# Latent attention rounds: the order of the values' products, the projection piece and the reading of its bank

## The chip, the cores and the metric

The kernel runs on one core of one Trainium2 chip. The metric is the device time of one launch in microseconds (us); lower is better. The core has a matrix engine (TensorE, "PE" in the profile; its weight loads are "PEld"), VectorE (DVE), ScalarE (ACT), GpSimd (POOL) and SyncE (SP), which issues most of the DMAs. Each engine works through its own queue in order, and the engines wait for each other on semaphores. Matrix products land in PSUM, which has 8 banks of 512 fp32 columns.

## The reference

One launch computes two blocks on a sequence of 1024 tokens of 1024 features: a first block (a gated recurrence, a band attention, a feed-forward layer), and a second one (a recurrent layer, and then a latent attention). Only the latent attention matters here. Cut to what is needed:

```python
c_kv = rms_norm(ckr[..., :256], kv_norm)               # latent of keys and values
k_nope = einsum("bsc,chd->bshd", c_kv, w_uk)           # 8 heads of 128
v      = einsum("bsc,chd->bshd", c_kv, w_uv)           # 8 heads of 128
q = einsum("bsc,chd->bshd", c_q, w_uq)                 # 8 heads of 128 + 64; c_q has 384 features
q_rope = apply_rope(q[..., 128:], cos, sin)
s = (q_nope . k_nope + q_rope . k_rope) * ATTN_SCALE   # causal, in blocks of 128 queries
p = softmax(s)
y = (p @ v) * silu(gate)
out = x + y @ w_out
```

## The kernel before

The latent attention runs in 64 rounds, one for each head H = n // 8 and block of 128 queries. In a head the blocks go backwards: round r = n % 8 has 8 - r key blocks of 128 keys. The projections of keys, queries and values for two heads (a pair) are cut into 14 pieces, and the pieces of the next pair are spread over the rounds of the present one, as "fillers" between the products of the attention (`MLA_FILLERS`, line 70, `mla_fillers`, line 73). In an even head rounds 1 to 4 have one filler each: pieces 10 to 13. An odd head below 7 has one or two in every round: 14; 15 and 16; 17; 18; 19; 20; 21 and 22; 23. The last head has none. So four heads (0, 2, 4, 6) are of the even kind with fillers, and three (1, 3, 5) of the odd kind. Pieces 14 and 15 are the rotary part of the queries, 10, 11, 16 and 17 the other part of the queries, 12, 13, 18 and 19 keys, 20 to 23 values (counted from the pair's first piece; in the code m is that number plus 14 for each earlier pair).

Each engine has its order written out by hand (PE from line 1624, ACT from 2319, DVE from 3267). In round n:

- PE: `mla_transposed(n)` (line 1583, the weights of block n turned by nk transposes into banks 4 and 5); where there are two fillers, the first one; `mla_scores(n + 2)` (lines 1564 to 1573, into banks 0 and 1 or 2 and 3); the last filler, `mla_projection` (lines 1507 to 1509 and, for values, 1547 to 1549, into bank 7); `mla_values(n - 1)` (line 1593, into bank 6).
- DVE: `mla_probs_copied(n)` (line 3239, out of banks 4 and 5); the first of two fillers is read; `mla_max(n + 2)` (3228); `mla_read` of the last filler; `mla_inverse(n + 2)` (3233, a reciprocal of a sum that ACT forms in `mla_exp`); `mla_gated(n - 1)` (3250, out of bank 6). In rounds 2 and 3 of the odd heads `mla_rope_turned` follows (3214 to 3217), in round 4 of the odd and round 1 of the even heads `mla_rope_low` (2362, from the q_rope tile).
- ACT: in round 4 of the odd and round 1 of the even heads `mla_rope_high` (2281) goes first; the first of two fillers; `mla_exp(n + 2)` (2299); `mla_high` of the last filler (2274: it reads bank 7 and writes the rounded high part of a key or query piece; the pieces of values and of the rotary part have none); `mla_normed(n + 2)` (2305).

`mla_read` of a key or query piece (2362) waits for `mla_high` of that piece, since it forms the difference of bank and high part; of a value piece (3208) and a rotary piece (3199) it is a plain copy that waits for PE alone.

The waits that the change touches, all of PE:

```python
            def mla_projection(m):
                ...
                elif m >= 10:
                    pe.wait_ge(s_pread, m)
...
            def mla_transposed(n):
                pe.wait_ge(s_normed, n + 1)
                ...
                await_at_least(pe, mla.copied, n)
...
            def mla_values(n):
                pe.wait_ge(mla.copied, n + 1)
                await_at_least(pe, mla.outL, n)
```

`s_pread` counts the pieces that DVE has read: a piece from number 10 on goes into bank 7, and so waits until DVE has read the piece before it. `mla.copied` counts `mla_probs_copied`, and `mla.outL` counts `mla_gated`, so the values' product of block n waits until bank 6 has been read for block n - 1.

Of the kernel before, what the change touches and what calls it, by code (L numbers as in the profile page):

```python
# [72 lines left out]
def mla_fillers(n):  # L73

    H, r = n // 8, n % 8
    return [PIECES * (H // 2) + i for i in MLA_FILLERS[H % 2][r]] if H < 7 else []
# [129 lines left out]
def half_of(h):  # L206
    return slice(h * HALF, (h + 1) * HALF)
# [24 lines left out]
def await_at_least(eng, semaphore, count):  # L232

    if not isinstance(count, int) or count > 0:
        eng.wait_ge(semaphore, count)


def fused_kernel(nc, a):
    ctx = ExitStack()
    with ctx:  # L240
# [749 lines left out]
        def mla_key_columns(n):  # L990

            nk = mla.items[n][2]
            return 5 * P // 2 if nk == 5 else min(HALF, nk * P)
# [7 lines left out]
        def mla_bank(m):  # L1001
            return (4, 5, 6, 7, 0, 1, 4, 5, 6, 7)[m] if m < 10 else 7

        def mla_done(m):

            return MM_PER_UNIT * (K_UNIT + 3 * (m // PIECES)) + MLA_COUNT[m % PIECES]
# [12 lines left out]
        def _(pe):  # L1019
# [532 lines left out]
            def mla_scores(n):  # L1552
                H, j, nk = mla.items[n]
                e = H % 2
                if n % 8 < 2:
                    pe.wait_ge(s_pread, 6 if H == 0 else PIECES * (H // 2) + (PIECES if e else 6))
                await_at_least(pe, mla.probed, n - 1)
                queries = slice(j * P, (j + 1) * P)
                for b in range((nk + 3) // 4):
                    k0, k1 = b * mla_key_columns(n), min((b + 1) * mla_key_columns(n), nk * P)  # L1560
                    bank = 2 * (n % 2) + b
                    out = ps[:, bank, 0:k1 - k0]
                    diagonal = k1 == nk * P
                    nc.tensor.matmul(out, q_nopeH[:, e, queries], k_nopeH[:, e, k0:k1], start=True, stop=False)
                    nc.tensor.matmul(out, q_nopeL[:, e, queries], k_nopeH[:, e, k0:k1], start=False, stop=False)
                    nc.tensor.matmul(out, q_nopeH[:, e, queries], k_nopeL[:, e, k0:k1], start=False, stop=False)
                    if n % 8 < 2 and b == 0:
                        pe.wait_ge(s_qrL, H + 1)
                        pe.wait_ge(s_krL, 1)
                    nc.tensor.matmul(out, q_ropeS[:, e, queries], k_ropeH[:, 0, k0:k1], start=False, stop=False)  # L1570
                    last = nc.tensor.matmul(out, q_ropeS[:, e, queries], k_ropeL[:, 0, k0:k1], start=False, stop=not diagonal)
                    if diagonal:
                        last = nc.tensor.matmul(ps[:, bank, k1 - k0 - P:k1 - k0], ident_r[:], causal_r[:], start=False, stop=True)
                last.then_inc(mla.scored, 1)

            def mla_transposed(n):
                nk = mla.items[n][2]
                pe.wait_ge(s_normed, n + 1)
                if n == 0:
                    pe.wait_ge(s_pread, 8)  # L1580
                await_at_least(pe, mla.copied, n)
                for k in range(nk):
                    last = nc.tensor.transpose(transposed_flat[:, k * P:(k + 1) * P], mla.probs[:, n % 2, k * P:(k + 1) * P], ident[:])
                last.then_inc(mla.transposed, 1)

            def mla_values(n):
                H, _, nk = mla.items[n]
                if n % 16 == 0:
                    pe.wait_ge(s_pread, PIECES * (n // 16) + 10)
                pe.wait_ge(mla.copied, n + 1)  # L1590
                await_at_least(pe, mla.outL, n)
                for k in range(nk):
                    last = nc.tensor.matmul(ps[:, 6, 0:P], v_mla[H // 2 % 2][:, k, (H % 2) * P:(H % 2 + 1) * P],  # L1593
                                            mla.probsT[:, n % 2, k * P:(k + 1) * P], start=(k == 0), stop=(k == nk - 1))
                last.then_inc(mla.summed, 1)
# [10 lines left out]
            def output_chunks(r, first, last):  # L1606
                u, (_, tok) = STAGE["wob"][0] + r, output_half(r)
                if first == 0:
                    pe.wait_ge(s_split, u + 1)
                    if r > 4:  # L1610
                        pe.wait_ge(*output_read.at(r - 3))
                for k in range(first, last):
                    c = Y_ORDER[k]
                    if r % DC == 0:
                        pe.wait_ge(s_y7l, k + 1 + (r // DC) * 4 * (k >= 4))
                    wH, wL = w_high[:, u % 2, c * P:(c + 1) * P], w_low[:, u % 2, c * P:(c + 1) * P]
                    out = ps[:, output_bank(r)]
                    nc.tensor.matmul(out, wH, y7H[:, c, tok], start=(k == 0), stop=False)
                    nc.tensor.matmul(out, wH, y7L[:, c, tok], start=False, stop=False)
                    done = nc.tensor.matmul(out, wL, y7H[:, c, tok], start=False, stop=(k == DC - 1))  # L1620
                if last == DC:
                    done.then_inc(s_mm, MM_PER_UNIT)

            for n in range(64):
                fillers = mla_fillers(n)
                mla_transposed(n)
                if len(fillers) == 2:
                    mla_projection(fillers[0])
                if n + 2 < 64:
                    mla_scores(n + 2)  # L1630
                if fillers:
                    mla_projection(fillers[-1])
                if n:
                    mla_values(n - 1)
                if n >= 62:
                    output_chunks(0, 2 * n - 124, 2 * n - 122)
            mla_values(63)
# [722 lines left out]
        def _(dve):  # L2360
            def low_of(L, source, H):
                return nc.vector.tensor_tensor(L, source, f32(H), ALU.subtract)
# [830 lines left out]
            def mla_read(m):  # L3193

                p, i = m // PIECES, m % PIECES
                t, h, bank = i // 10, i % 2, ps[:, mla_bank(m)]
                if i in (0, 1):
                    dve.wait_ge(s_mm, mla_done(m))
                    nc.vector.tensor_copy(q_rope[:, half_of(i)], bank).then_inc(s_pread, 1)
                elif i in (2, 3, 10, 11, 4, 5, 12, 13):  # L3200
                    H, L = (q_nopeH, q_nopeL) if i in (2, 3, 10, 11) else (k_nopeH, k_nopeL)
                    dve.wait_ge(s_qnH, 8 * p + {2: 1, 3: 2, 4: 3, 5: 4, 10: 5, 11: 6, 12: 7, 13: 8}[i])
                    low_of(L[:, t, half_of(h)], bank, H[:, t, half_of(h)]).then_inc(s_pread, 1)
                else:
                    r = 2 * (i - 6)
                    dve.wait_ge(s_mm, mla_done(m))
                    await_at_least(dve, mla.summed, 16 * (p - 1))
                    nc.vector.tensor_copy(v_mla[p % 2][:, r:r + 2].rearrange("p r n -> p (r n)"), bank).then_inc(s_pread, 1)
# [37 lines left out]
            def mla_gated(m):  # L3246
                H, j, _ = mla.items[m]
                dve.wait_ge(mla.summed, m + 1)
                y = cgate[:, H, j * P:(j + 1) * P]
                nc.vector.tensor_tensor(y, ps[:, 6, 0:P], y, ALU.mult).then_inc(mla.outL, 1)  # L3250
# [16 lines left out]
            for n in range(64):  # L3267
                fillers = mla_fillers(n)
                H, r = n // 8, n % 8
                mla_probs_copied(n)  # L3270
                if len(fillers) == 2:
                    mla_read(fillers[0])
                if n + 2 < 64:
                    mla_max(n + 2)
                if fillers:
                    mla_read(fillers[-1])
                if n >= 62:
                    y_low_of(2 * n - 120)
                    y_low_of(2 * n - 119)
                if n + 2 < 64:  # L3280
                    mla_inverse(n + 2)
                if n:
                    mla_gated(n - 1)
                if H % 2 and H < 7 and r in (2, 3):
                    mla_rope_turned(H // 2 + 1, r - 2)
                if H % 2 == 0 and r == 1 or H % 2 and H < 7 and r == 4:
                    mla_rope_low(H + 1)
                if 57 <= n < 60 or n == 61:
                    y_low_of(min(n - 57, 3))
# [169 lines left out]
```

## Time and profile before

| | |
|---|---|
| median of 3 runs | 2532.97 us (2532.96 to 2535.27) |
| profiled execution, its own time | 2535.13 us |
| its span, first to last instruction | 2533.2 us |
| PE busy | 2484.3 us, 98% of the span |
| DVE busy | 1621.2 us, 64% |
| ACT busy | 946.6 us, 37% |
| chain that ended last | PE 82%, DVE 11%, ACT 3% |
| granted TensorE clock, mean | 0.996 of full speed |

Matmuls are pipelined: the record of one overlaps the start of the next, so the time from one start to the next is what counts on PE. The records of a 128-column fp32 product in line 1593 come in two passes (16 records for 8 key blocks).

### The profile page before, as it was taken

The numbers are of one execution on the slowest core, as the hardware profiler recorded it, in microseconds if no ns is written. First come the engines' busy times: TensorE is split into PE (matmuls) and PEld (weight loads), VectorE is DVE, ScalarE is ACT, GpSimd is POOL, SyncE is SP. The second block draws the span as 40 slices with busy tenths as digits, with TensorE's granted clock in tenths as the row PEclk, the third lists the DMA queues.
The fourth block names the chain that finished last, engine by engine and source line by source line (L and its number), as shares of the span: only waits on it lengthen the run. The fifth ranks groups of instructions, "written<-read, shape, count | busy, mean of one in ns | idle before, by whom it ended". The sixth has DMA issues, their size and how long they took to land.

```text
span 2533.2 us, 33765 instructions
## 1 busy us (share of the span) xinstructions
PE 2484.3 (98%) x13036; PEld 2071.5 (82%) x13036; DVE 1621.2 (64%) x1977; ACT 946.6 (37%) x1369; POOL 1055.7 (42%) x769
## 2 busy tenths in 40 slices
PE   8999999999999989999999999999999999999998
PEld 7878888887788878888878878888888888888887
DVE  6685723476655687667688796677784552556565
ACT  6252223222322343333345454346551331444432
POOL 3454523211243378888871113243345333111135
PEclk9999999999999999999999999999999999999999
DMA  3111121211341122222277521311132311110133
GB/s 143 45 35 34 47 72 42 71 39 47 130 165 62 55 75 75 84 92 75 84 210 195 152 68 67 112 42 41 49 116 75 133 67 49 29 29 10 34 117 125
DMA packets 65381, 201.96 MB, mean 80 GB/s; under 512 B 7136, under 2 KB 16480, under 8 KB 63840
## 3 DMA queue, kind: packets, MB, share of 16 engines
q1 hardware_dynamic: 52080, 152.85, 17.8%
q10 hardware_dynamic: 6256, 35.73, 3.7%
q0 software_dynamic: 6912, 11.54, 2.8%
q8 instruction: 91, 1.49, 0.2%
q14 instruction: 42, 0.34, 0.0%
HBM read 159.20 MB, written 32.51 MB: 76 GB/s over the span
## 4 chain that ended last, share of the span: by engine, by line
PE 82%; DVE 11%; ACT 3%; issue 2%; DMA 1%; POOL 1%; ACTq 0%; DVEq 0%; SPq 0%; POOLq 0%
PE ps L1034 8%; PE ps L1036 8%; PE ps L1035 8%; PE ps L1110 6%; PE ps L1112 5%; PE ps L1111 5%; PE ps L1373 5%; PE ps L1374 5%; PE ps L1375 5%; PE ps L1434 2%; PE ps L1436 2%; PE ps L1435 2%; PE ps L1593 2%; PE ps L1292 1%; PE ps L1309 1%
## 5 line engine op out<-in xcount | busy, mean ns | idle before, releaser
L767 POOL TENSOR_TENSOR derived_vectors<-w_staged 1x1 f32<-1x1 f32 x146 | 35.1, 240 | 1170.6 <-PE ps L1036 479.5
L772 POOL TENSOR_TENSOR w_low<-w_staged,w_high 128x1024 fp32r<-128x1024 f32 x146 | 390.3, 2673 | 11.4
L1110 PE MATMUL ps<-h_mix_high,w_high 128*128 128x512 f32 x688 | 278.5, 405 | 0.0
L1112 PE MATMUL ps<-h_mix_high,w_low 128*128 128x512 f32 x688 | 269.6, 392 | 0.0
L1111 PE MATMUL ps<-h_mix_low,w_high 128*128 128x512 f32 x688 | 269.3, 391 | 0.0
L1112 PEld LDWEIGHTS ps<-h_mix_high,w_low 128*128 128x128 f32 x688 | 129.7, 188 | 27.9
L1110 PEld LDWEIGHTS ps<-h_mix_high,w_high 128*128 128x128 f32 x688 | 130.0, 189 | 26.0 <-issue 0.2
L1111 PEld LDWEIGHTS ps<-h_mix_low,w_high 128*128 128x128 f32 x688 | 130.0, 189 | 25.2
L768 POOL CAST w_high<-w_staged 128x1024 fp32r<-128x1024 f32 x146 | 150.5, 1031 | 0.0
L1034 PE MATMUL ps<-h_rnn_high,w_high 128*128 128x512 f32 x320 | 124.6, 389 | 1.4 <-DVE h_rnn_low L2384 1.4
L2828 DVE TENSOR_TENSOR squares<-ps,squares 128x512 f32<-128x512 f32 x84 | 57.8, 689 | 106.3 <-PE ps L1375 105.6
L1035 PE MATMUL ps<-h_rnn_low,w_high 128*128 128x512 f32 x320 | 124.5, 389 | 0.0
L1036 PE MATMUL ps<-h_rnn_high,w_low 128*128 128x512 f32 x320 | 124.5, 389 | 0.0
L1434 PE MATMUL ps<-act_block_high,w_high 128*128 128x512 f32 x308 | 120.4, 391 | 2.0 <-DVE w_low L2759 1.4
L1436 PE MATMUL ps<-act_block_high,w_low 128*128 128x512 f32 x308 | 119.9, 389 | 0.0
L1435 PE MATMUL ps<-act_block_low,w_high 128*128 128x512 f32 x308 | 119.8, 389 | 0.0
L1881 ACT ACTIVATE probs_band<-ps,softmax_stats 128x640 f32<-128x640 f32 (+4 forms) x64 | 42.4, 663 | 142.1 <-DVE softmax_stats L2684 125.2
L2835 DVE TENSOR_TENSOR squares<-squares,rstd 128x512 f32<-128x512 f32 x66 | 90.8, 1378 | 3.9 <-ACT rstd L1692 1.8
L2299 ACT ACTIVATE probs_mla<-ps,softmax_stats 128x1024 f32<-128x1024 f32 (+3 forms) x64 | 47.5, 742 | 105.8 <-DVE softmax_stats L3228 97.9
L1593 PE MATMUL ps<-probs_mla_T,v_mla 128*128 128x128 f32 x576 | 76.0, 277 | 1.6 <-DVE mla_gate L3250 1.2
L1593 PEld LDWEIGHTS ps<-probs_mla_T,v_mla 128*128 128x128 f32 x576 | 71.8, 191 | 6.1 <-issue 3.1
L2690 DVE COPY probs_band_T<-ps 128x640 f32<-128x640 f32 (+4 forms) x64 | 42.1, 657 | 49.4 <-PE ps L1300 49.1
(632 smaller groups left out, 7084.2 us busy)
## 6 DMA issues: line engine op xcount, KB each, us to landing
w_staged<-weights_in SPq DMA_DIRECT2D x168, 512.0 KB, 3.5
w_staged_late<-weights_in SPq DMA_DIRECT2D x22, 512.0 KB, 4.3
gates_loaded<-gates ACTq DMA_DIRECT2D x8, 1024.0 KB, 7.2
gates<-tmp SPq DMA_DIRECT2D x16, 512.0 KB, 2.6
act_raw<-gates SPq DMA_DIRECT2D x16, 512.0 KB, 7.3
gates<-gates_staged_late SPq DMA_DIRECT2D x22, 256.0 KB, 2.0
x_in<-xT_in SPq DMA_DIRECT2D x8, 512.0 KB, 8.2
x_mid<-xT_in ACTq DMA_DIRECT2D x1, 4096.0 KB, 15.1
```

The lines of the kernel that those rows point to most:

```text
L768: nc.gpsimd.tensor_copy(w_high[:, j], w_staged[:, j]).then_inc(s_wh, 1)
L772: nc.gpsimd.tensor_tensor(w_low[:, j], w_staged[:, j], f32(w_high[:, j]), ALU.subtract).then_inc(s_split, 1)
L1034: nc.tensor.matmul(ps[:, bank], wH, rhs[0][:, r, tok], start=(n == 0), stop=False)
L1035: nc.tensor.matmul(ps[:, bank], wH, rhs[1][:, low_r, tok], start=False, stop=False)
L1036: last = nc.tensor.matmul(ps[:, bank], wL, rhs[0][:, r, tok], start=False, stop=last_chunk)
L1110: nc.tensor.matmul(ps[:, bank], wH, h1H[:, c, tok], start=(c == 0), stop=False)
L1111: nc.tensor.matmul(ps[:, bank], wH, h1L[:, c, tok], start=False, stop=False)
L1112: done = nc.tensor.matmul(ps[:, bank], wL, h1H[:, c, tok], start=False, stop=(c == DC - 1))
L1434: nc.tensor.matmul(ps[:, bank], wH[:, columns], H[:, c], start=not added and c == 0, stop=False, skip_group_check=added)
L1435: before_last = nc.tensor.matmul(ps[:, bank], wH[:, columns], L[:, c], start=False, stop=False, skip_group_check=added)
L1436: last = nc.tensor.matmul(ps[:, bank], wL[:, columns], H[:, c], start=False, stop=c == chunks - 1, skip_group_check=added)
L1593: last = nc.tensor.matmul(ps[:, 6, 0:P], v_mla[H // 2 % 2][:, k, (H % 2) * P:(H % 2 + 1) * P], mla.probsT[:, n % 2, k * P:(k + 1) * P], st ...
```

## The change

PE: the values' product of the block before follows the scores directly, and the last filler comes behind it, at the end of the round. DVE: the last filler is read behind the reciprocal and the gating, instead of ahead of them. ACT's order stays as it is: `mla_exp(n + 2)`, `mla_high` of the last filler, `mla_normed(n + 2)`. Where a round has two fillers, the first keeps its place on all three engines. `mla_rope_turned` and `mla_rope_low` follow the reading on DVE. No instruction is added or removed, and no wait is changed.

```diff
@@ PE @@
                 if n + 2 < 64:
                     mla_scores(n + 2)
+                if n:
+                    mla_values(n - 1)
                 if fillers:
                     mla_projection(fillers[-1])
-                if n:
-                    mla_values(n - 1)
                 if n >= 62:
                     output_chunks(0, 2 * n - 124, 2 * n - 122)
@@ DVE @@
                 if n + 2 < 64:
                     mla_max(n + 2)
-                if fillers:
-                    mla_read(fillers[-1])
                 if n >= 62:
                     y_low_of(2 * n - 120)
                     y_low_of(2 * n - 119)
                 if n + 2 < 64:
                     mla_inverse(n + 2)
                 if n:
                     mla_gated(n - 1)
+                if fillers:
+                    mla_read(fillers[-1])
                 if H % 2 and H < 7 and r in (2, 3):
                     mla_rope_turned(H // 2 + 1, r - 2)
```

## Rows read from the trace of the kernel before

**Rows 1.** Windows, heads 2 and 3: stretch, length, busy time by engine, PE clock.

```profile
2232.41:2263.66 31.25, 30.91 (x208) 28.14 (x206) 18.41 (x38) 15.63 (x29) 7.08 (x6) 1.00 0.08 24
2263.66:2306.28 42.62, 41.42 (x273) 37.56 (x273) 25.40 (x50) 16.63 (x30) 3.57 (x3) 1.00 0.10 26
```

**Rows 2.** Waits, all rounds: waiting, waited for, total us, times, longest.

```profile
PE ps L1547 <- DVE k_nope_low L2362: 2.8, 3, 0.9
```

**Rows 3.** Timeline, head 3, rounds 0 and 1: start, length, instruction.

```profile
2268.55 0.38 PE L1593 MATMUL ps<-probs_mla_T,v_mla 128*128 128x128 f32 x2
2268.75 0.69 DVE L3199 COPY q_rope<-ps 128x512 f32<-128x512 f32 x1 [1.19 <-PE ps L1509]
...
2269.50 0.50 PE L1507 MATMUL ps<-cq_high,w_high 128*128 128x512 f32 x1
```

**Rows 4.** Timeline, head 3, rounds 2 to 4: two turns, copies, ACT between them.

```profile
2282.68 0.71 PE L1583 MATMUL ps<-identity,probs_mla 128*128 128x128 f32 x5
...
2283.09 0.68 DVE L3214 TENSOR_TENSOR q_rope_rotated<-q_rope_rotated,cos_sin 128x512 f32<-128x512 f32 x1
...
2285.02 0.82 DVE L3239 COPY probs_mla_T<-ps 128x640 f32<-128x640 f32 x1
...
2286.91 0.59 ACT L2274 ACTIVATE k_nope_high<-ps 128x512 fp32r<-128x512 f32 x1
...
2287.53 0.69 DVE L2362 TENSOR_TENSOR k_nope_low<-ps,k_nope_high 128x512 fp32r<-128x512 f32 x1 [1.23 <-ACT k_nope_high L2274]
...
2290.32 0.68 DVE L3239 COPY probs_mla_T<-ps 128x512 f32<-128x512 f32 x1
2290.44 1.06 ACT L2281 ACTIVATE q_rope_split<-q_rope 64x1024 fp32r<-64x1024 f32 x1 [1.50 <-DVE q_rope L3217]
```

**Rows 5.** Timeline, head 3, rounds 4 to 6: up to piece 21.

```profile
2291.85 0.58 ACT L2274 ACTIVATE k_nope_high<-ps 128x512 fp32r<-128x512 f32 x1
...
2292.47 0.69 DVE L2362 TENSOR_TENSOR k_nope_low<-ps,k_nope_high 128x512 fp32r<-128x512 f32 x1 [1.13 <-ACT k_nope_high L2274]
2293.07 0.15 DVE L3233 RECIPROCAL softmax_stats<-softmax_stats 128x1 f32<-128x1 f32 x1
...
2293.45 1.22 DVE L2362 TENSOR_TENSOR q_rope_split<-q_rope,q_rope_split 64x1024 fp32r<-64x1024 f32 x1
...
2294.70 0.56 DVE L3239 COPY probs_mla_T<-ps 128x384 f32<-128x384 f32 x1
...
2295.98 0.17 DVE L3233 RECIPROCAL softmax_stats<-softmax_stats 128x1 f32<-128x1 f32 x1
...
2296.11 0.39 PE L1547 MATMUL ps<-w_high,ckv_high 128*128 128x256 f32 x1
...
2296.25 0.41 DVE L3239 COPY probs_mla_T<-ps 128x256 f32<-128x256 f32 x1
```

**Rows 6.** Timeline, head 2, round 1: the gating and the piece behind the scores.

```profile
2237.40 0.27 DVE L3250 TENSOR_TENSOR mla_gate<-ps,mla_gate 128x128 f32<-128x128 f32 x1
...
2237.66 0.45 PE L1507 MATMUL ps<-cq_high,w_high 128*128 128x512 f32 x1
```

**Rows 7.** Timeline, head 2: values behind a piece (round 2); rounds 5 and 6.

```profile
2245.59 1.72 PE L1593 MATMUL ps<-probs_mla_T,v_mla 128*128 128x128 f32 x14
...
2255.09 0.49 PE L1583 MATMUL ps<-identity,probs_mla 128*128 128x128 f32 x3
...
2256.98 0.38 PE L1583 MATMUL ps<-identity,probs_mla 128*128 128x128 f32 x2
```

**Rows 8.** Timeline, head 7: values behind scores, behind the gating, and line 1618 behind values.

```profile
2420.56 1.77 PE L1593 MATMUL ps<-probs_mla_T,v_mla 128*128 128x128 f32 x14
...
2426.66 0.27 DVE L3250 TENSOR_TENSOR mla_gate<-ps,mla_gate 128x128 f32<-128x128 f32 x1
...
2427.08 1.35 PE L1593 MATMUL ps<-probs_mla_T,v_mla 128*128 128x128 f32 x10 [0.27 <-DVE mla_gate L3250]
...
2435.04 0.48 PE L1618 MATMUL ps<-y_mla_high,w_high 128*128 128x512 f32 x1
```

## The prediction

> **What bounds the kernel now.** I began with the page's busy times: PE is busy 98% of the span, so at most 2% can be won anywhere, and what is lost must show as a wait of PE. The chain of waits gives PE 82% and DVE 11%, so there are places where DVE's queue, not PE, sets the time. The next view was the stretches, cut at the heads [rows 1]: an even head takes 31.25 us with PE busy 30.91, an odd one 42.62 us with 41.42. The even rounds are bound by PE almost to the last 0.3 us; the odd ones lose 1.20 us. The waits of PE [rows 2] name the largest part: the products of a value piece wait for DVE's reading of a key piece, 0.9 us, once in each of the three odd heads. The last view, the timeline of one odd head [rows 3 to 5], shows why: in rounds 2 to 4 DVE must turn the rotary part of the queries twice (from 2283.09 to 2285.02, 1.93 us each) and form its low part (from 2293.45 to 2294.70, 1.25 us), and falls behind PE.
>
> **What is moved, and where it lands.** Nothing is added or removed, so PE's and DVE's sums of work stay. In a round with a filler the values' product goes ahead by the piece's length, and the piece ends just ahead of the next round's transposes. ACT and DVE can read the piece only from there on, while their other work of the round is done earlier. So DVE begins each next round late, and where the next piece comes first in its round (pieces 15 and 21, the first of two fillers), only the transposes lie between the end of one piece and the start of the next one in the same bank 7; before, the values' product lay there too. I work the odd head through, then the even one.
>
> *Odd head, round 0 to 1.* Before, piece 14 ends at 2268.55, the reading starts 0.20 later and lasts 0.69, and piece 15 starts at 2269.50, 0.06 after its end [rows 3]: already just at the limit. After, two records (0.22 us from 2268.55) of values' product go ahead of piece 14, which so ends at 2268.77, plus 0.08 for changed neighbours (below): 2268.85. Reading, 0.20 + 0.69 + 0.06, puts piece 15 at 2269.80 instead of 2269.50: +0.30. Rounds 1 and 2 are bound by PE and cost only their 0.08 each, so the transposes of round 3, before at 2282.68 [rows 4], come at 2283.14: +0.46.
>
> *Odd head, round 2 to 6.* From the end of piece 17, which now is that moment, E = 2283.14, DVE and ACT run one chain, in which no step waits for PE. Its links, each from start to start: piece to ACT's high part 0.20 (as in rows 3); high part to reading 0.62; reading 0.60; the turn 1.93; copy, maximum, exponential to the high part of piece 18 1.89; reading 0.62, then 0.60; the second turn 1.93; ACT's high rotary part starts 0.12 after the copy of round 4, and the high part of piece 19 1.41 after that; reading 0.62, then 0.60; the low rotary part 1.25; copy of round 5 to the reciprocal 1.28; reciprocal and gating 0.27; reading of piece 20 and release 0.74. [rows 4, 5] Sum 14.68 us: piece 21 starts at 2297.82 instead of 2296.11, +1.71 us. Before, the reading of piece 20 stood ahead of the reciprocal, so the copy of round 5, the maximum, the exponential and the reciprocal were not all in front of it. The values' products that are now early fill the old 0.9 us wait, but PE then waits longer in the same stretch: for the gating ahead of the values of block 27, for the copies ahead of the transposes of rounds 5 and 6, and last for piece 20's reading. These waits lie inside the 14.68 us and are not added. Rounds 6 and 7 have value pieces, which ACT doesn't touch; they cost 0.10 each. An odd head: +1.9 us, three of them +5.7.
>
> *Even head.* In round 1 the values' product now directly follows the scores, at 2237.66, but the gating that frees bank 6 ends at 2237.67 [rows 6]. The last head, which has no fillers, shows this wait: the gating ends at 2426.93 and PE resumes at 2427.08, 0.15 later, and the product takes some 0.08 longer [rows 8] (the 0.08 is an estimate from its records, 1.35 us for 10). Before, the piece lay over it. That is 0.15 + 0.08, +0.03 for the piece behind it. Head 0 has no block before its round 1's product to wait for and is spared the first two. Rounds 2 to 4: 0.08 each. In round 5, which has no piece, transposes, scores and values take PE 1.89 us (2255.09 to 2256.98) [rows 7]; the copy that the transposes of round 6 wait for now comes behind piece 13's reading: 0.20 + 0.62 + 0.60, a copy of 384 columns 0.56, release 0.15, together 2.13 us [rows 3 to 5, 8]. It is 0.24 late, with 0.04 to restart: 0.28. An even head: 0.26 + 0.24 + 0.28 = +0.78; head 0 some 0.6. Four: +3.0.
>
> *Changed neighbours.* The 14 records of a values' product take 1.72 us behind a piece and 1.77 behind scores [rows 7, 8]; the first product of a 512-column piece takes 0.45 behind scores [rows 6], and its nearest kin behind values, line 1618, 0.48 [rows 8]. Hence 0.05 + 0.03 = 0.08 in each of the rounds bound by PE (16 in even heads, 5 in each odd one). The trace has no piece behind values, so this is bounded: below by 0 (the turnover is paid at another seam either way), above by 0.15, the size of a release, so 31 rounds cost between 0 and 4.7 us, and 2.5 as taken. It is the row nearest to the case that I take.
>
> *Queues moved past.* The pieces 11, 13 and 15 free weight buffers for POOL and SP. Piece 11 and 13 end later by one values' product at most, 1.6 us, and their successors are needed rounds later (a round is 42.62 / 8 = 5.3 us on average in an odd head [rows 1]); nothing. ACT's normalisation stands behind the high part of the now later piece. It is needed only by the transposes two rounds on, a round away: nothing, unless ACT also falls behind, which I keep in the range.
>
> Sum: 5.7 + 3.0 = +8.7 us. The profiled execution took 2535.13 us with a span of 2533.2, some 2 us above the median of the runs; a difference of this kind carries over, so the forecast is 2532.97 + 8.7 = 2541.7 us.
>
> **Rivals.** (a) *The values fill the stall.* If the later reading did not reach PE, the odd heads would get back their idle time: 42.62 - 41.42 = 1.20 each, 3.6 in all, 2529.4 us: not slower. It decides if the chain from piece 17 to piece 21 is not 14.68 but under 12.97 (2296.11 less 2283.14), and it brings the whole 1.20 from 11.8 down. For it speaks that PE's one long wait [rows 2] has a product ready to go there. Against it, every link of the chain is a duration from the rows, and the program's order leaves none out. 4%. (b) *Only part of it bites.* The seams cost nothing and the even heads' waits are absorbed: 1.3 to 1.7 for each odd head or the even losses alone, 3 to 5 us, 2536 to 2538. For: the even waits are a tenth or two each. 17%. (c) *More bites.* DVE's lateness is handed on round by round, through ACT's normalisation or the maximum, as one more exponential in each chain (about 1 us in seven heads on top): 2545 to 2549. 7%. (d) *The clock.* The granted clock is 1.00 in both kinds of head, with 1.20 us of idle PE in the odd [rows 1]. The changed odd head has some 3 us of it in a stretch of 15 us. If the clock fell from 2.4 to 1.2 GHz there, the work from piece 21 to the head's end, 2296.11 to 2306.28, would double: +10 for each odd head, +30, some 2572. 2%.
>
> The Trainium skill, "TensorE: Matmul & The Clock Gate", section "A second HAM failure mode: psum-queue depth-cycling", says that short idle times between groups of matmuls that cycle through PSUM banks can make the clock swing. By that rule (d) would come true; the trace so far disagrees, since the rounds already have such pauses at 1.00.
>
> **How the numbers follow.** The forecast, 2538.1 to 2545 us, has 70%. What this kernel's measurement can tell from no change is about 0.2%, 5.07 us. Faster by that much takes more than the whole idle time of all odd heads, so 2%. Within it: (a), (b), less the part for faster, 19%. Slower: the forecast, (c) and (d), 79%. The range: its lower end in (b), where even the odd heads lose only half of what I reckon, 2535.5; its upper end in (c), with the seams at their upper bound, 2546.5. It leaves out (a), (d) and the ends of (b) and (c).
>
> **What would show it.** In the new trace: piece 15 starts some 0.3 us further from the head's start; piece 20 no longer waits for a key piece's reading, but piece 21 waits over 1 us for v_mla's copy; an odd head takes 44.2 to 44.7 us, an even one 31.8 to 32.2, and the last head is as it was; a new wait of values' products for mla_gate in round 1 of heads 2, 4 and 6 and in round 4 of the odd ones; PE's busy sum is unchanged within 1 us. The prediction is wrong if the odd heads take 42.6 us or less, if the even heads lose more than the odd ones, or if the loss lies outside the rounds.

## The result

The changed kernel takes 2540.31 us (median of 10 runs, 2539.04 to 2540.94) against 2533.09 us for the kernel before (10 runs, 2532.68 to 2535.27): ratio 1.0026, 95% interval 1.0018 to 1.0034. It is slower by 7.2 us; 8.7 had been forecast. The profiled executions took 2540.68 and 2535.13 us, with spans of 2538.8 and 2533.2. Among the executions behind this document one was slow, a run of experiment 7 that took 3545.32 us at a mean granted clock of 0.655, for a cause that is not known; the comparisons are of the others.

The profile after, heads 2 and 3 and the last head, cut at the same transposes as in [rows 1] (stretch, length, busy time by engine, PE clock):

```profile
2233.75:2265.38 31.63, 31.21 (x209) 28.03 (x207) 18.07 (x38) 15.25 (x29) 7.07 (x6) 1.00 0.08 23
2265.38:2309.56 44.18, 41.80 (x273) 37.15 (x274) 25.16 (x49) 16.15 (x30) 3.52 (x3) 1.00 0.09 25
...
2416.95:2442.30 25.35, 23.50 (x169) 21.37 (x170) 18.61 (x39) 18.04 (x32) 0.00 (x0) 1.00 0.18 65
```

An even head grew from 31.25 to 31.63 us, an odd one from 42.62 to 44.18, and the last, which has no fillers, is as before (25.34 then). Over all heads, start to start: even 0.20, 0.38, 0.38 and 0.35 us more, odd 1.59, 1.56 and 1.58, together 6.04 us. The clock stayed at 1.00. That the rest of the 7.2 is scatter outside the rounds is taken up in the last section.

The waits of PE in the whole stretch of the rounds (waiting, waited for, total us, times, longest):

```profile
PE ps L1547 <- DVE v_mla L3208: 3.5, 3, 1.2
PE ps L1583 <- DVE probs_mla_T L3239: 2.7, 6, 0.6
PE ps L1593 <- DVE mla_gate L3250: 2.6, 10, 0.5
PE ps L1583 <- ACT probs_mla L2305: 0.9, 4, 0.2
```

The wait of [rows 2] is gone. In its place stand, in each odd head, a wait of 1.2 us for piece 20's reading, one of 0.6 us for a copy (ahead of the transposes of round 5), and two for the gating, 0.27 us in round 4 and 0.19 in round 5.

The chain from piece 17 to piece 21 in the timeline of head 3, to be laid beside [rows 4, 5] (start, length, instruction, idle before):

```profile
2284.56 0.71 PE L1583 MATMUL ps<-identity,probs_mla 128*128 128x128 f32 x5
2284.76 0.60 ACT L2274 ACTIVATE q_nope_high<-ps 128x512 fp32r<-128x512 f32 x1 [1.94 <-PE ps L1509]
...
2285.39 0.69 DVE L2362 TENSOR_TENSOR q_nope_low<-ps,q_nope_high 128x512 fp32r<-128x512 f32 x1 [2.19 <-ACT q_nope_high L2274]
...
2286.00 0.68 DVE L3214 TENSOR_TENSOR q_rope_rotated<-q_rope_rotated,cos_sin 128x512 f32<-128x512 f32 x1
...
2287.93 0.81 DVE L3239 COPY probs_mla_T<-ps 128x640 f32<-128x640 f32 x1
...
2289.81 0.59 ACT L2274 ACTIVATE k_nope_high<-ps 128x512 fp32r<-128x512 f32 x1
...
2290.43 0.69 DVE L2362 TENSOR_TENSOR k_nope_low<-ps,k_nope_high 128x512 fp32r<-128x512 f32 x1
2290.44 1.35 PE L1593 MATMUL ps<-probs_mla_T,v_mla 128*128 128x128 f32 x10 [0.27 <-DVE mla_gate L3250]
...
2292.97 0.68 DVE L3239 COPY probs_mla_T<-ps 128x512 f32<-128x512 f32 x1
2293.08 1.06 ACT L2281 ACTIVATE q_rope_split<-q_rope 64x1024 fp32r<-64x1024 f32 x1 [2.18 <-DVE q_rope L3217]
...
2293.80 0.52 PE L1583 MATMUL ps<-identity,probs_mla 128*128 128x128 f32 x3 [0.63 <-DVE probs_mla_T L3239]
...
2294.50 0.58 ACT L2274 ACTIVATE k_nope_high<-ps 128x512 fp32r<-128x512 f32 x1
...
2295.83 1.22 DVE L2362 TENSOR_TENSOR q_rope_split<-q_rope,q_rope_split 64x1024 fp32r<-64x1024 f32 x1
...
2298.36 0.16 DVE L3233 RECIPROCAL softmax_stats<-softmax_stats 128x1 f32<-128x1 f32 x1 [0.53 <-ACT probs_mla L2299]
...
2298.63 0.68 DVE L3208 COPY v_mla<-ps 128x512 f32<-128x512 f32 x1
...
2299.36 0.38 PE L1547 MATMUL ps<-w_high,ckv_high 128*128 128x256 f32 x1 [1.17 <-DVE v_mla L3208]
```

Each reading (2285.39, 2290.43) now starts only after the transposes of the next round have begun, and a turn and a copy stand behind it. From 2284.56 to 2299.36 it is 14.80 us.

### The profile page after: what moved, and what is told of

The parts are those of the page before. It is cut to its first block, busy times and chain, and to the rows that moved or that the text cites. A ratio compares the mean times of both kernels' runs of the same rounds, so it can differ in the third digit from the quotient of the medians.

```text
span 2538.8 us, 33765 instructions
## 1 busy us (share of the span) xinstructions
PE 2486.0 (98%) x13036; PEld 2069.4 (82%) x13036; DVE 1615.8 (64%) x1977; ACT 942.4 (37%) x1369; POOL 1055.7 (42%) x769
## 4 chain that ended last, share of the span: by engine, by line
PE 81%; DVE 12%; ACT 3%; issue 3%; POOL 1%; DMA 0%; ACTq 0%; DVEq 0%; SPq 0%; POOLq 0%
PE ps L1034 8%; PE ps L1035 8%; PE ps L1036 8%; PE ps L1110 5%; PE ps L1112 5%; PE ps L1111 5%; PE ps L1373 5%; PE ps L1375 5%; PE ps L1374 5%; PE ps L1434 2%; PE ps L1436 2%; PE ps L1435 2%; PE ps L1593 2%; PE ps L1292 1%; PE ps L1309 1%
```

## The experiments

In all experiments, a head's length is the time from its first transpose to that of the next head; it repeats within 0.06 us over the heads of one kind in every trace, so it tells tenths of a microsecond apart where whole times scatter by two. The kernel before was run again beside the experiments, and each ratio goes against its own such runs: a median of 2534.78 us for experiments 1 to 4, 2533.35 for 5 to 8. Head 0 is left out of "even": its values' product of round 1 has no earlier gating to wait for.

| | odd head | even head | ratio to before, 95% interval |
|---|---|---|---|
| before | 42.6 | 31.25 | |
| changed | 44.18 | 31.63 | 1.0026 (1.0018 to 1.0034) |
| 1 PE's order alone | 45.0 | 33.78 | 1.0066 (1.0052 to 1.0080) |
| 2 VectorE's order alone | 44.05 | 31.35 | 1.0018 (1.0009 to 1.0028) |
| 3 before, turn ahead | 40.55 | 31.25 | 0.9974 (0.9963 to 0.9984) |
| 4 changed, turn and low part ahead | 42.14 | 31.66 | 0.9999 (0.9990 to 1.0008) |
| 5 changed, piece 20 read as before | 43.3 | 31.64 | 1.0019 (1.0010 to 1.0028) |
| 6 changed, normalisation first on ScalarE | 45.8 | 31.64 | 1.0043 (1.0030 to 1.0057) |
| 7 as 4 and 5 together | 42.15 | 31.64 | 1.0005 (0.9996 to 1.0014) |
| 8 as 3, the change in five rounds of sixteen | 40.54 | 31.49 | 0.9980 (0.9971 to 0.9989) |

### 1 and 2: each half of the change alone

```diff
# experiment 1: PE as changed, VectorE as before
+                if n:
+                    mla_values(n - 1)
                 if fillers:
                     mla_projection(fillers[-1])
-                if n:
-                    mla_values(n - 1)
```

> PE's part of the change alone: the values' product ahead of the last filler; VectorE keeps the old order, reading ahead of reciprocal and gating. Theory (PE is held by how long after the piece's end VectorE frees bank 6, bank 7 and the copies): the gating now stands behind a reading that can't start before the round's end, so the next values' product waits for it: piece end + 0.20 + 0.62 + 0.60 + 0.07 + 0.27 + 0.15 = 1.91 us, against transposes and scores of 1.88, 1.47, 1.10 and 0.95 us in rounds 2 to 5 of an even head: some 2.2 us of waits there, +2.4 an even head; odd heads +1.4 to 1.6 (piece 21 is reached by a chain of about the same length); together +14 us, and thus worse than the whole change. Rival (the moved products themselves cost, VectorE's part is harmless or a loss): +5 to +7, as the whole change or less.

```diff
# experiment 2: VectorE as changed, PE as before
-                if fillers:
-                    mla_read(fillers[-1])
...
                 if n:
                     mla_gated(n - 1)
+                if fillers:
+                    mla_read(fillers[-1])
```

> VectorE's part alone: the last filler read behind reciprocal and gating; PE keeps the old order. Theory: the gating waits for the values' product, which here is behind the piece, so the reading waits for that too. Even heads: the copy of round 5's block ends 2256.78 on the scale of before, needed at 2256.98: 0. Odd heads: piece 15 starts 0.4 us late, piece 21 about 1.0 us late: +1.4 each, together +4.3 us, nearly all in the odd heads. Rival (VectorE's order alone is the whole loss): +6 with even heads at +0.38. Rival (it is nothing without PE's part): within 1 us.

Measured: PE's order alone adds 2.4 us to each odd head and 2.53 to an even one, 2551.94 us in all against 2534.78 (+17). The waits of its PE in the rounds:

```profile
PE ps L1593 <- DVE mla_gate L3250: 15.7, 22, 1.2
PE ps L1547 <- DVE v_mla L3208: 1.7, 3, 0.6
```

The even heads were forecast within 0.15; the odd ones lost 2.4 for 1.4 to 1.6. There PE waits for the gating in rounds 3, 4 and 5, by 0.28, 1.25 and 1.24 us, on top of the 0.57 for bank 7 in round 6, and rounds 3 to 6 grew by 0.46, 0.87, 0.26 and 0.48 us; the expectation had counted the way to piece 21 alone. VectorE's order alone adds 1.44 to each odd head, as forecast, and 0.10 to an even one, where 0 had been forecast. So the halves don't add up to the whole: 2.4 + 1.4 in the odd heads, but 1.57 together, and 2.53 + 0.10 in the even, but 0.38. Reading late is a loss by itself, but with the values' product early it keeps bank 6's gating from being late as well, and so it is the lesser evil.

### 3 and 4: the turn out of the chain

```diff
# experiment 3: the kernel before, the turn ahead of the reading
+                if H % 2 and H < 7 and r in (2, 3):
+                    mla_rope_turned(H // 2 + 1, r - 2)
                 if fillers:
                     mla_read(fillers[-1])
...
-                if H % 2 and H < 7 and r in (2, 3):
-                    mla_rope_turned(H // 2 + 1, r - 2)
```

> The kernel before, with one move: in rounds 2 and 3 of the odd heads VectorE turns the rotary part ahead of reading the last filler, while it would idle for ScalarE's high part (2 us of idle there). Theory (the turn on the chain from piece 17 to piece 21 is what PE waits for): the 1.2 us idle of PE in each odd head goes: 41.3 to 41.5 us instead of 42.6, -3.6 to -4 us in all, even heads unchanged. Rival (other links take its place, the low rotary part or the copies): under 1 us gained.

```diff
# experiment 4: the changed kernel, turn and low rotary part ahead of the reading
                 if n:
                     mla_gated(n - 1)
-                if fillers:
-                    mla_read(fillers[-1])
                 if H % 2 and H < 7 and r in (2, 3):
                     mla_rope_turned(H // 2 + 1, r - 2)
                 if H % 2 == 0 and r == 1 or H % 2 and H < 7 and r == 4:
                     mla_rope_low(H + 1)
+                if fillers:
+                    mla_read(fillers[-1])
```

> The changed kernel with the turn (rounds 2 and 3 of the odd heads) and the low rotary part (round 4 odd, round 1 even) put ahead of the reading of the last filler. Theory: the chain from piece 17 to piece 21 loses two turns; what is left is piece 20's reading behind reciprocal and gating: piece 21 starts some 0.7 us earlier than in the kernel before, odd heads 41.9 to 42.1 us instead of 44.2, even heads stay at 31.6: about -1 us against before, 6 to 7 us better than the change. Rival (the loss is in the order of PE's products or in piece 20's reading alone): at least +3 against before.

Measured: experiment 3 takes 2528.37 us against 2534.78, 6.4 us less (6.15 over the heads): the fastest kernel of this study, faster than both. Its heads 2 and 3 (columns as above):

```profile
2230.29:2261.54 31.25, 30.91 (x209) 28.15 (x207) 18.43 (x38) 15.61 (x29) 7.10 (x6) 1.00 0.08 24
2261.54:2302.09 40.55, 40.55 (x273) 37.33 (x273) 25.65 (x50) 16.70 (x30) 3.56 (x3) 1.00 0.10 27
```

PE is busy for the whole of the odd head. What counts is the length: 2.07 us went, where the busy time of before had shown only 1.20 of idle time. In the kernel before VectorE stood idle for ScalarE's high part ahead of both readings, 2.06 us in round 2 and 1.23 in round 3; the turns now stand there. Experiment 4 shows the same on the changed kernel: 2.04 us less in each odd head, even heads as changed, and the loss against before gone (forecast 41.9 to 42.1, measured 42.14). The moved order still takes 1.6 us more than the other one (42.14 against 40.55), about as much as with the turns in the chain (44.18 against 42.62). That the two agree is chance, for the 1.6 us lie elsewhere, and experiment 4 moves one thing more than experiment 3. Stage by stage 0.19 us are piece 15's stall in round 1 and 0.8 the wait ahead of piece 21. The other 0.6 lie in round 5: the low rotary part, 1.22 us, which experiment 4 alone puts ahead of piece 19's reading, now holds that reading and with it piece 20:

```profile
2290.31 1.22 DVE L2362 TENSOR_TENSOR q_rope_split<-q_rope,q_rope_split 64x1024 fp32r<-64x1024 f32 x1
2291.56 0.69 DVE L2362 TENSOR_TENSOR k_nope_low<-ps,k_nope_high 128x512 fp32r<-128x512 f32 x1
...
2292.31 0.39 PE L1547 MATMUL ps<-w_high,ckv_high 128*128 128x256 f32 x1 [0.32 <-DVE k_nope_low L2362]
```

What the changed kernel gains by the turns alone was not run.

### 5 and 7: piece 20's reading

```diff
# experiment 5: the changed kernel; experiment 7: the same on top of experiment 4
+                if fillers and r == 5:
+                    mla_read(fillers[-1])
...
-                if fillers:
+                if fillers and r != 5:
                     mla_read(fillers[-1])
```

> The changed kernel, but in round 5 of the odd heads VectorE reads the last filler (piece 20) where it did before, ahead of reciprocal and gating. Theory: piece 21 waits for that reading, and the reading for exponential, reciprocal and gating; without them it starts 0.86 us earlier (2298.50 for 2299.36 in the trace of the change), so odd heads 43.3 us for 44.18, even heads unchanged 31.63: 2.6 us better than the change, 3.5 worse than before. Rival (the whole of the odd heads' loss is the turn's chain, and the copy that the transposes wait for comes last anyway): odd heads stay at 44.2.

> The changed kernel with the turn and the low rotary part ahead of the reading (as run before, odd heads 42.14 us), and in round 5 of the odd heads piece 20 read ahead of reciprocal and gating. Theory: with VectorE on time the reading already starts 0.20 us after the piece's end, and what is left (0.6 us at piece 21) is the turnaround of bank 7: end of the piece to release 0.94 us, less transposes of two blocks: nothing gained, 42.1 us. Rival (reciprocal and gating ahead of the reading are the cost wherever it stands): 0.4 to 0.9 us less in each odd head.

Measured: in experiment 5 the odd heads take 43.3 us, 0.88 less than changed (forecast 0.86), and PE's wait at piece 21 falls from 1.2 to 0.3 us. Over all heads that is 3.5 us more than before, as forecast; the whole times say 5.0 (2538.34 against 2533.35), with scatter outside the rounds. In experiment 7 nothing changes, 42.15 for 42.14. The timeline of experiment 4 says why; piece 20 ends where the transposes start, at 2293.84:

```profile
2293.84 0.38 PE L1583 MATMUL ps<-identity,probs_mla 128*128 128x128 f32 x2
2294.04 0.69 DVE L3208 COPY v_mla<-ps 128x512 f32<-128x512 f32 x1 [0.25 <-PE ps L1549]
2294.65 0.41 DVE L3239 COPY probs_mla_T<-ps 128x256 f32<-128x256 f32 x1
2294.79 0.39 PE L1547 MATMUL ps<-w_high,ckv_high 128*128 128x256 f32 x1 [0.57 <-DVE v_mla L3208]
```

VectorE is free and idle for 0.25 us before the reading, so its place in the order no longer counts. What is left at this place, 0.57 us, is bank 7 itself: 0.95 us from the end of piece 20 to the start of piece 21, with only two transposes to fill it.

### 6: ScalarE's order

```diff
+                if n + 2 < 64:
+                    mla_normed(n + 2)
                 if fillers:
                     mla_high(fillers[-1])
-                if n + 2 < 64:
-                    mla_normed(n + 2)
```

> The changed kernel, with ScalarE's normalisation put ahead of the high part of the last filler, which now comes late. Theory (the high part is a link of the chain, the normalisation is not): in rounds 3 and 4 of the odd heads the high part must then wait for reciprocal and normalisation, 0.95 and 0.75 us: odd heads 45.9 us for 44.18, even heads the same, +5 against the change. Rival (the normalisation behind the late high part holds the transposes): odd and even heads shorter than in the change.

Measured: odd heads 45.8, +1.6 on the change, even heads the same. In rounds 3 and 4 the high part starts behind reciprocal and normalisation, and rounds 4 and 5 grow by 0.84 and 0.74 us. ScalarE's high part is a link of the chain, the normalisation is needed only two rounds on: the order that ScalarE kept was the right one for the change.

### 8: the moved order where nobody waits

```diff
# on top of experiment 3: PE
+                late = n % 16 in (2, 3, 4, 9, 15)
...
+                if n and late:
+                    mla_values(n - 1)
                 if fillers:
                     mla_projection(fillers[-1])
-                if n:
+                if n and not late:
                     mla_values(n - 1)
# VectorE (late as above)
-                if fillers:
+                if fillers and not late:
                     mla_read(fillers[-1])
...
                 if n:
                     mla_gated(n - 1)
+                if fillers and late:
+                    mla_read(fillers[-1])
```

> The kernel before with the turn ahead of the reading (odd heads 40.56 us, even ones 31.25), and the change on PE and VectorE in rounds 2, 3, 4 of the even heads and 1 and 7 of the odd ones alone. Theory (the moved order costs nothing between other neighbours; it costs where someone waits for a late reading): even heads 31.50, by the one wait of the transposes of round 6 for the copy behind piece 13's reading; odd heads 40.56. Rival (each moved product costs 0.08 us, as the prediction took): even heads 31.74, odd heads 40.72.

Measured: 31.49 and 40.54 us. Moving the values' product ahead of the piece costs nothing by itself, in five rounds of sixteen: the seams of the prediction would have made 31.74 and 40.72. The even heads' 0.24 is the one wait that had been worked out. There is no gain in it either.

## Why the prediction held, point by point

The mechanism held; its size did not quite. The rounds lost 6.04 us for the 8.7 forecast. The medians differ by 7.2, and that they come so near the forecast is in part luck: about 1.2 us of it lie outside the rounds.

- *Where the time goes.* As predicted: the odd heads carry most, the even ones a little, the last head nothing; the new waits are the ones named, at piece 21, for the copies and for the gating; one more for the gating, 0.19 us in round 5 of the odd heads, was not named. The half of it that could be tested by undoing it was: experiments 4 and 5.
- *Rounds 0 to 3 of an odd head.* Forecast +0.46, measured +0.16 from the first transpose to those of round 3. Piece 15's stall is 0.20 of it (a round of 8.55 us for 8.35; forecast 0.22 without the seams); the rest of the forecast was seams.
- *Chain from piece 17 to piece 21.* Forecast 14.68, measured 14.80; the difference is one link, from piece 19's reading to the low rotary part, 0.72 us (2295.11 to 2295.83) for 0.60. Piece 21 comes 1.53 us further from the head's start than before (forecast 1.71).
- *Rounds 6 and 7.* Forecast +0.20, measured +0.03: seams again. An odd head: +1.9 forecast, +1.58 measured; its 44.16 to 44.20 us just touch the 44.2 to 44.7 that were to be seen.
- *Even heads.* Forecast +0.78 each and 0.6 in head 0, measured 0.38, 0.38, 0.35 and 0.20; at 31.63 us they stayed under the 31.8 to 32.2 that were to be seen. The two waits were right: round 1 grew by 0.16 and round 5 by 0.24 (forecast 0.15 and 0.24 before their additions for a restart). The gating and the held product, to be laid beside [rows 6, 8]:

```profile
2238.72 0.27 DVE L3250 TENSOR_TENSOR mla_gate<-ps,mla_gate 128x128 f32<-128x128 f32 x1
2239.14 2.02 PE L1593 MATMUL ps<-probs_mla_T,v_mla 128*128 128x128 f32 x16
2240.92 0.47 PE L1507 MATMUL ps<-cq_high,w_high 128*128 128x512 f32 x1
```

  From 2238.99 to 2239.14 it is the 0.15 of the last head; but the product then takes 1.78 us, as it did behind a piece. The restart's 0.08 wasn't there.
- *The step that was mis-sized: the changed neighbours.* 31 seams at 0.08 made 2.5 us of the 8.7; measured, nothing. Rounds 2 to 4 of the even heads took 5.56, 4.27 and 3.67 us before and 5.55, 4.25 and 3.65 after, and experiment 8 says the same. Records had been compared by their length (1.77 for 1.72, 0.48 for 0.45), one side of the seam only. From start to start the same round shows:

```profile
2244.95 1.77 PE L1593 MATMUL ps<-probs_mla_T,v_mla 128*128 128x128 f32 x14
2246.48 0.48 PE L1507 MATMUL ps<-cq_high,w_high 128*128 128x512 f32 x1
```

  14 records in 1.53 us here against 1.56 in the order of before, and the piece 2.15 against 2.12 behind scores: what one neighbour takes, the other gives back. The lower bound of the prediction was the right end. Without seams and restarts its sum would have been about 5.8 (4.4 from the odd heads, 1.4 from the even ones), against 6.04 measured in the rounds.
- *Rivals.* That the early values fill the old stall happened (piece 20 waits no more), and didn't help, as argued. Its price, 1.20 us for an odd head, was read from busy times and was too low: 2.07 was there to be had (experiment 3). Of (b) one half came true, the seams that cost nothing; the even heads' waits were not absorbed. The clock (d) did not fall: it was 1.00 in the odd head with 2.38 us of idle in 44.18, and 1.00 in experiment 6 with 3.4 in 45.75. The Trainium skill ("TensorE: Matmul & The Clock Gate", section "A second HAM failure mode: psum-queue depth-cycling") has a kernel whose clock swung with short idle times while it cycled through PSUM banks; the traces here don't show it.
- *Its own test on busy time* failed by a little: PE's busy sum rose by 1.7 us (2486.0 for 2484.3) where 1 was allowed. No instruction was added. The likely reason, not tested: records of PE overlap and their ends are modelled, so where a wait parts two of them more of both is counted; heads 2 and 3, which both gained waits, show 0.30 and 0.38 us more.

## What to carry to other kernels

Before a product is moved up on the matrix engine, follow who reads the one that it is moved past: that one now ends at the end of the round, and everything its reader has behind it in its queue starts late. Where an engine idles for another's result and then has other work behind it, put that work into the idle time: one call moved on VectorE gave 6.4 us, where the moved products cost 7.2. Estimate seams from start to start over both neighbours, never from the lengths of records of one.

## What was not expected of the hardware

**Busy time hides short waits of PE.** Before, an odd head showed PE busy for 41.42 of 42.62 us and one listed wait of 0.9, yet 2.07 us could be won. Waits of two or three tenths lie under the modelled ends of the records before them. They show when a round is laid beside the same round of another trace: rounds 4, 5 and 6 took 4.21, 4.48 and 6.52 us from transposes to transposes, and 3.66, 3.32 and 6.17 in experiment 3.

**The scatter of whole times is outside these rounds.** The first transpose came at 2158.49 us in the trace of before and at 2155.82 in that of experiment 5, with the same code up to there. Part of it is the granted clock in one stretch near the start. The windows of the kernel before, then those of experiment 5:

```profile
160.00:165.00 5.00, 2.41 (x46) 1.84 (x45) 5.00 (x6) 1.25 (x2) 2.54 (x3) 0.96 0.33 105
165.00:170.00 5.00, 5.00 (x37) 4.17 (x36) 5.00 (x6) 2.23 (x3) 4.92 (x4) 0.50 0.01 3
```

```profile
160.00:165.00 5.00, 2.43 (x65) 1.90 (x63) 5.00 (x6) 1.28 (x2) 2.72 (x2) 1.00 0.34 105
165.00:170.00 5.00, 5.00 (x31) 4.13 (x28) 5.00 (x6) 2.21 (x3) 4.92 (x4) 1.00 0.01 3
```

Behind the same idle time of PE, half of the first five microseconds, the clock was at 0.50 (1.2 GHz) in one execution and at 1.00 (2.4 GHz) in the other. Experiment 5 is the only one of the ten traces with 1.00 there: four show 0.50, five 0.66 to 0.68. Up to this stretch they are within 0.5 us of it; at 191 us they stand 2.3 to 2.7 us and 1.0 to 1.2 us behind it. But the clock there is not the whole scatter: by the first transpose other differences have mixed the groups, and the five with 0.66 to 0.68 stand anywhere from 0.8 to 2.7 us behind.

The ten runs of the kernel before fall into two clusters, about 2533 us (six) and 2535 (four), of which its profile shows the slower; of the changed kernel two runs lie at 2539.1 and eight at 2540.2 to 2540.9. Cluster against cluster the difference is 6.1 and 5.4 us, near the 6.04 of the rounds. Most runs of the one kernel are in the lower cluster and most of the other in the upper, and this would make up the 7.2 between the medians. That the clusters come from the clock near the start was not shown.
